# The compressed branch's steps one take earlier in a two-block fp32 layer kernel

## The chip, the cores and the metric

One NeuronCore of a Trainium2 chip runs the whole program. The metric is the device time of one execution in microseconds; for several executions the median is given.

## The reference

256 tokens of width 1024 pass a first block and then two layers of a second kind. All is float32.

```python
def first_block(x, ...):
    h = rms_norm(x, norm_mix_g)
    (f_q, f_k, f_v, f_f, n_q, k_c, v_c, k_s, v_s, k_w, v_w, n_g, g_a, g_b) = split_cols(h @ w_in)
    out_a = from_heads(fox_attention(qa, ka, va, log_f)) @ w_fox_up          # 8 heads, forget gates
    kc = rms_norm(compress_blocks(k_c, cmp_k_w1, cmp_k_w2, cmp_k_pos), nsa_k_g)
    vc = compress_blocks(v_c, cmp_v_w1, cmp_v_w2, cmp_v_pos)
    out_b = from_heads(nsa_attention(qb, kc, vc, ks_, vs_, kw_, vw_, gates)) @ w_nsa_up
    x = x + (sigmoid(g_a) * out_a + sigmoid(g_b) * out_b) @ w_out
    return x + hierarchical_moe(rms_norm(x, norm_ffn_g), ...)                # 16 experts, 2 of one group of 4

def compress_blocks(t, w1, w2, pos):      # t: (B,S,G,dh); 15 overlapping blocks of 32 tokens, stride 16
    blk = t[:, idx] + pos[None, None, :, None, :]
    return gelu(blk.reshape(B, G, n_cmp, 32 * dh) @ w1) @ w2
```

nsa_attention adds three branches with sigmoid gates: over the compressed keys, over selected blocks (at 256 tokens all blocks are selected), and over a window. The second block has two hybrid layers (a gated linear recurrence and a sliding-window attention).

## The kernel before, in words

**Takes and pieces.** The weights lie in HBM as half panels of 128x2048 (1 MB). SP loads them in a fixed order into a ring of four slots (`sp_program`, L532); load n waits until all that was read from load n - 4 is used. A half panel is cut into four pieces of 128x512. ScalarE makes each piece's high part (`copy` into `w_hi`, L1955) and VectorE its low part (`tt` into `w_lo`, L414), so that TensorE can multiply in three passes (`mm3`, L541 to L543). Two pieces are one take: take t uses pieces 2t and 2t + 1, and `feed(2 * t + AHEAD)` with AHEAD = 9 makes all pieces up to number 2t + 8 during take t. A `w_hi` buffer comes free through `taken`.

Takes 0 to 23 (T_Z) compute the columns of the first projection in six panels of four takes, with tokens on the partitions: tile 0 (tokens 0 to 127) in bank 0 and tile 1 in bank 1. In panel 0 TensorE runs the four takes for tile 0 first and then the four for tile 1. At the end of a panel ScalarE copies bank 0 to `zin` (`out_free[0]`, which TensorE waits for before the next panel) and VectorE bank 1. Takes 24 to 39 (T_GATE) are 24 matmuls each, 256 columns wide; takes 40 to 47 multiply with the two up matrices; takes 48 to 55 with w_out; then come the routing and the experts.

**What is done beside the takes.** `beside_block1` (L162) lists, for each take, the small steps that run on every engine in that take: attention blocks ("jobs") with scores, weigh, turn and values, and the steps 0 to 12 of the compressed branch. `ATT_1` gives each job's takes; job 6 has its scores in take 27, job 7 in 29, job 8 in 31, job 9 in 33, job 10 in 35, job 11 in 37, with weigh and turn two takes on and values two more. Per take, the engines run:

- TensorE: the take's matmuls, then the steps in the order of the list (`behind`, L1070);
- VectorE: first `log_in`, `weigh` and `scores_out` of this take, then the feed, then the rest (`behind`, L1840). `weigh_now` is the same function as `weigh` in this last part;
- ScalarE: the feed, `turn_out`, `scores_out` (the exponentials), the copy of a finished pair of gate rows, then the rest (`behind`, L2228). Each engine works strictly through its list and stands at every wait;
- GpSimd: small roots (`rstd_pow`, L426).

Two raw halves of each of the compressed branch's two first matrices come through the ring too, as loads 18, 19, 21 and 22. Loads 22 and 23 wait for `cmp_mm` 3, loads 25 and 26 for `cmp_mm` 4; load 21 waits for the four pieces of load 17 (68 to 71).

**The compressed branch.** TensorE's `compress` (L737), VectorE's (L1407), ScalarE's (L2056) and GpSimd's (L2384) share the step numbers; all of TensorE's use bank 7. TensorE raises `cmp_mm` after every step but 2.

- 0 and 1: TensorE transposes the raw keys (0) and values (1) into bank 7; VectorE copies them in four pieces to `kv2` (L1412) and raises `cmp_v`. TensorE's step 1 waits for `cmp_v` 1. Step 0 waits for `side` 9, set by `nsa_side` 3 of take 26.
- 2: VectorE adds the positions in eight instructions into `blk` (in `buf_d`), which GpSimd has zeroed (`cmp_z`).
- 3 and 4: TensorE multiplies the blocks with the first and second half of w1, 32 matmuls each (L757).
- 4 on ScalarE: GELU of the sum. 5: transposes. 6: second matrices (L770), VectorE's norm with GpSimd's root. 7: the key side. 8: scores (L780), softmax on VectorE and ScalarE. 9, 10: transposes of the probabilities, waiting for `cmp_f` of `cmp_weigh`. 11, 12: the values (L795).

`fx` and `fsum` (forget gates by pair of heads, used in takes 12 to 20) lay in `buf_d`, so the zeroing had to wait for the last forget-attention block. `buf_b` is first written otherwise by `nsa_side` 0 in take 22.

Of the kernel before, what the change touches and what calls it, by code (L numbers as in the profile page):

```python
# [14 lines left out]
P = 128  # L15
S = 256
# [3 lines left out]
HD = 64  # L20
# [66 lines left out]
FOX_JOBS, L1_JOBS = 4, 12  # L87
# [74 lines left out]
def beside_block1():  # L162
    table = {3: [("lower", 0)], 5: [("fox_sums", 0)], 7: [("fox_norms", 0)], 9: [("fox_sums", 1), ("fox_q", 0)],
             11: [("forget", 0), ("fox_norms", 1)], 12: [("log_in", 0), ("nsa_gates", 0)], 13: [("fox_k", 0)],
             20: [("win_sums", 0)], 21: [("win_norms", 0)], 22: [("nsa_side", 0), ("nsa_side", 1)],
             23: [("nsa_side", 2)], 24: [("slc_sums", 0)], 25: [("slc_norms", 0)], 26: [("nsa_side", 3)]}
    at_takes(table, list(enumerate(ATT_1)))
    for take, step in ((28, 0), (29, 1), (30, 2), (31, 3), (34, 4), (35, 5), (36, 6), (37, 7), (38, 8), (39, 9),
                       (40, 10), (41, 11), (42, 12)):
        table.setdefault(take, []).append(("compress", step))  # L170

    for take, job in ((31, 7), (39, 11)):
        table[take].remove(("weigh", job))
    table[30].insert(table[30].index(("compress", 2)), ("weigh_now", 7))
    table[38] += [("weigh_now", 11), ("cmp_weigh", 0)]
    for take, name, arg in ((39, "gate_on", 0), (41, "gate_on", 1), (43, "up_split", 0)):
        table.setdefault(take, []).append((name, arg))
    return table
# [55 lines left out]
def build(nc, panels, x_in, prm_in, lay_in, pre_in, post_in, c0_in, c1_in, c2_in, out):  # L234
    ctx = ExitStack()
    with ctx:
        V, A, T, G = nc.vector, nc.scalar, nc.tensor, nc.gpsimd
        pe, dve, act, pool, sp = Queue(T), Queue(V), Queue(A), Queue(G), Queue(nc.sync)
# [32 lines left out]
        buf_b = sb("buf_b", 1024)  # L271
        at_k = col()
        keys = sb("keys", 2560)
        buf_c = sb("buf_c", 2048)
        buf_d = sb("buf_d", 2048)
# [18 lines left out]
        ps = ctx.enter_context(nc.psum_tensor("ps", [P, 8, 512], F32))  # L294
# [22 lines left out]
        g_row = buf_a[:, :]  # L317
        slc_k = zin[:, TT * ZA:TT * ZA + S]
        ntri = c1("ntri")
        fx, fsum = buf_d[:, 0:2 * P], buf_d[:, 2 * P:2 * P + S]  # L320
        cq = stat[:, 112:128].rearrange("p (a h) -> p a h", a=TT)
        ng = stat[:, 128:176].rearrange("p (a c h) -> p a c h", a=TT, c=3)
        kv2 = buf_c[:, 0:1024].rearrange("p (c g t) -> p c g t", c=2, g=2)
# [12 lines left out]
        def sem(name):  # L336
# [26 lines left out]
        value_mm, value_out, value_hi = sem("value_mm"), sem("value_out"), sem("value_hi")  # L363
        cmp_mm, cmp_v, cmp_a, cmp_z, cmp_blk, cmp_ms, cmp_rs, cmp_n, cmp_s, cmp_f = (
            sem("cmp_" + n) for n in ("mm", "v", "a", "z", "blk", "ms", "rs", "n", "s", "f"))
# [777 lines left out]
        def dve_program():  # L1143
# [247 lines left out]
            def cmp_weigh(_):  # L1391
# [12 lines left out]
                settle()  # L1404
                tt(sc3, sc3, bc(fc, CMP_PAD), ALU.mult).then_inc(cmp_f, 1)

            def compress(step):  # L1407
                if step in (0, 1):
                    dve.wait_ge(cmp_mm, step + 1)
                    for g in range(2):  # L1410
                        for jp in range(2):
                            i = V.tensor_copy(kv2[jp * HD:(jp + 1) * HD, step, g, 0:S - jp], ps[g * HD:(g + 1) * HD, 7, jp:S])  # L1412
                    i.then_inc(cmp_v, 1)
                elif step == 2:
                    dve.wait_ge(cmp_v, 2)
                    dve.wait_ge(cmp_z, 2)
                    for c in range(2):
                        pos = prmc(("pos_k", "pos_v")[c])
                        for g in range(2):
                            even = kv2[:, c, g, :].rearrange("p (n m j) -> p m n j", n=16, j=2)[:, :, :, 0]  # L1420
                            tt(blk[c][:, 0:8, g, 0:N_CMP], even[:, :, 0:N_CMP], bc(pos[:, 0:8], N_CMP),
                               ALU.add).then_inc(cmp_blk, 1)
                            tt(blk[c][:, 8:16, g, 0:N_CMP], even[:, :, 1:N_CMP + 1], bc(pos[:, 8:16], N_CMP),
                               ALU.add).then_inc(cmp_blk, 1)
                elif step == 5:
                    dve.wait_ge(cmp_mm, 5)
                    V.tensor_copy(scr[:, 512:768], ps[:, 7, 0:256]).then_inc(cmp_v, 1)
                elif step == 6:
                    kcn, sq, ss = scr[0:64, 768:832], scr[0:64, 832:896], stat[0:64, 288:289]
                    dve.wait_ge(cmp_mm, 6)  # L1430
                    for g in range(2):
                        V.tensor_copy(vc_bd[g * 32:(g + 1) * 32, g * HD:(g + 1) * HD], ps[g * 32:(g + 1) * 32, 7, 64:128])
                    V.tensor_copy(kcn, ps[0:64, 7, 0:64]).then_inc(cmp_v, 1)
                    dve.wait_ge(cmp_v, 4)
                    dv(tt(sq, kcn, kcn, ALU.mult))
                    settle()
                    dv(V.tensor_reduce(ss, sq, AX, ALU.add))
                    settle()
                    rstd_in(ss, ss, HD).then_inc(cmp_ms, 1)
                    dve.wait_ge(cmp_rs, 1)  # L1440
                    ts(kcn, kcn, ss, None, ALU.mult).then_inc(cmp_n, 1)
                elif step == 7:
                    dve.wait_ge(cmp_mm, 7)
                    for g in range(2):
                        i = ts(kc_bd[g * HD:(g + 1) * HD, g * 32:(g + 1) * 32], ps[0:64, 7, g * 32:(g + 1) * 32],
                               prmc("nk_g")[0:64, :], None, ALU.mult)
                    i.then_inc(cmp_v, 1)
                elif step == 8:
                    sc = scr[:, 1024:1536]
                    sc3 = sc.rearrange("p (h n) -> p h n", n=CMP_PAD)  # L1450
                    mx = stat[:, 320:336]
                    dve.wait_ge(cmp_mm, 8)
                    tt(sc, ps[:, 7, :], c1("cmp"), ALU.add).then_inc(cmp_v, 1)
                    dve.wait_ge(cmp_v, 6)
                    dv(V.tensor_reduce(mx, sc3, AX, ALU.max))
                    settle()
                    tt(sc3, sc3, bc(mx, CMP_PAD), ALU.subtract).then_inc(cmp_s, 1)
                elif step >= 11:
                    a = step - 11
                    dst = z3[:, a, ZNQ:ZNQ + 512]  # L1460
                    dve.wait_ge(cmp_mm, step)
                    dve.wait_ge(value_out, value_sums[a])
                    tt(dst, dst, ps[:, 7, :], ALU.add).then_inc(cmp_v, 1)
                    cmp_sums[0] += 1
# [352 lines left out]
            def pre_los(l, a, c):  # L1817
# [7 lines left out]
                     "slc_norms": lambda _: head_norms(HEADS_SLC, 4), "nsa_side": nsa_side, "qf_bound": qf_bound,  # L1825
                     "log_in": log_in, "scores_out": scores_out, "weigh": weigh, "weigh_now": weigh, "cmp_weigh": cmp_weigh, "values_out": values_out,
                     "up_split": up_split, "att_split": att_split, "hg_turn": hg_turn,
                     "compress": compress, "rope": rope, "swa_sides": swa_sides, "level": level, "head_norm": head_norm,
                     "head_scale": head_scale}

            def steps(t):
# [25 lines left out]
            for t in range(T_Z, T_GATE):  # L1857
                steps(t)
                i, step = divmod(t, 4)
# [15 lines left out]
            for t in range(T_UP, T_OUT):  # L1875
                which, i = divmod(t - T_UP, 4)
# [5 lines left out]
                g = [gates[:, (8 * n + 2 * i) * S:(8 * n + 2 * i + 2) * S] for n in range(2)]  # L1882
# [68 lines left out]
        def act_program():  # L1951
# [300 lines left out]
            for t in range(T_Z, T_GATE):  # L2252
                feed(2 * t + AHEAD)
                steps(t, "turn_out")
                i, step = divmod(t, 4)
                if step == 3:
                    n = Z_ORDER[i]
                    cols = PIECE if n < 5 else Z5
                    act.wait_ge(tok_mm, i + 1)
                    copy(z3[:, 0, n * 512:n * 512 + cols], ps[:, 0, 0:cols]).then_inc(out_free[0], 1)  # L2260
                steps(t, "scores_out")
                behind(t)
            for t in range(T_GATE, T_UP):
# [3 lines left out]
                if f:  # L2267
                    c = (4 * n + 2 * b) * S
# [3 lines left out]
            for t in range(T_UP, T_OUT):  # L2272
                which, i = divmod(t - T_UP, 4)
# [26 lines left out]
            for l in range(LAYERS):  # L2300
# [10 lines left out]
                for t in range(t0, t0 + L2_TAKES - 3):  # L2311
# [14 lines left out]
                    elif L_QF <= r < L_IH and (r - L_QF) % 2:  # L2326
                        j, n = divmod(r - L_QF, 8)
                        b = n // 2 % 2
                        c = (4 * j + 2 * b) * S
# [26 lines left out]
        def pool_program():  # L2356
# [10 lines left out]
            def norm_root(a):  # L2367
                pool.wait_ge(norm_ms, a + 1)
                rstd_pow(stat[:, 2 + a:3 + a]).then_inc(norm_rs, 1)
# [12 lines left out]
                    rstd_pow(stat[:, s0:s0 + TT * n]).then_inc(head_rs, 1)  # L2382

            def compress(step):  # L2384
                if step == 0:
                    pool.wait_ge(value_out, FOX_JOBS)
                    G.memset(buf_d[:, :], 0.0).then_inc(cmp_z, 1)
                    G.memset(buf_c[:, 1024:1216], 0.0).then_inc(cmp_z, 1)
                elif step == 6:
                    pool.wait_ge(cmp_ms, 1)  # L2390
                    rstd_pow(stat[0:64, 288:289]).then_inc(cmp_rs, 1)

# [20 lines left out]
            po(G.memset(minus_half[:, :], -0.5))  # L2413
            pool.wait_ge(po.sem, po.n)
            po(G.memset(fx, 0.0))
            norm_root(0)
            norm_root(1)
            feed(5)
# [204 lines left out]
```

## Time and profile before

| | us |
|---|---|
| median of 3 runs | 1034.82 |
| lowest, highest | 1032.77, 1040.07 |
| profiled execution, its time | 1036.86 |
| profiled execution, its span | 1035.1 |

The span runs from the first to the last instruction; the time is taken around it. In rows of a timeline, the columns are start and busy time in us, engine, line, operation, destination<-source and shape, count, and in brackets how long the engine had been idle and what ended that. Matmuls overlap, so the distance of two starts is what one costs, not its busy time. On VectorE and ScalarE successive starts overlap by about 0.1 us as well.

### The profile page before, as it was taken

What the parts mean: (1) busy time and instruction counts of PE and PEld (TensorE: products, weight loads), DVE (VectorE), ACT (ScalarE), POOL (GpSimd) and SP (SyncE); (2) the same over time, 40 slices, a digit from 0 to 9 for tenths busy, and PEclk for the clock granted to TensorE, in tenths of its full rate; (3) what the DMA queues carried; (4) which work ended last, traced back from release to release, by engine and by line L of the source; (5) the groups of instructions that cost most, each with busy time, mean ns of one, the idle gap of its engine ahead of it and who ended that gap; (6) DMA issues with size and microseconds to landing.
All of it is one profiled execution on the core that took longest, in us unless ns stands there. A gap on an engine that the chain in (4) does not pass through costs nothing.

```text
span 1035.1 us, 16491 instructions
## 1 busy us (share of the span) xinstructions
PE 1006.2 (97%) x6087; PEld 863.6 (83%) x6087; DVE 838.2 (81%) x1653; ACT 666.5 (64%) x1351; POOL 54.7 (5%) x48
## 2 busy tenths in 40 slices
PE   5999999999999999999999999999999999999997
PEld 4888878887887888877879999888887999988886
DVE  5889867867999999999979777796668887598584
ACT  5476555547889888897855676735456477753552
POOL 0202000002004020010000000000100000000010
PEclk9999999999999999999999999999999999999999
DMA  8543253333999999999964443333354434234321
GB/s 346 192 175 123 86 233 130 141 145 112 391 365 374 392 350 381 366 339 366 384 241 164 163 148 139 101 140 127 112 194 177 170 122 160 90 129 150 117 91 41
DMA packets 30178, 211.31 MB, mean 204 GB/s; under 512 B 3728, under 2 KB 3856, under 8 KB 5136
## 3 DMA queue, kind: packets, MB, share of 16 engines
q1 hardware_dynamic: 28368, 205.01, 53.2%
q10 hardware_dynamic: 1728, 5.21, 1.3%
q8 instruction: 51, 0.84, 0.3%
q14 instruction: 31, 0.25, 0.1%
HBM read 209.16 MB, written 1.05 MB: 203 GB/s over the span
## 4 chain that ended last, share of the span: by engine, by line
PE 72%; DVE 15%; DMA 6%; ACT 4%; issue 2%; POOL 0%; ACTq 0%; DVEq 0%; POOLq 0%; SPq 0%
PE ps L541 19%; PE ps L543 18%; PE ps L542 18%; DVE w_lo L414 10%; DMA ring<-in_panels 5%; PE ps L1023 4%; PE ps L546 4%; PE ps L703 2%; PE ps L733 2%; ACT w_hi L1955 1%; DMA g_in<-in_prm 1%; PE ps L1011 1%; PE ps L757 1%; DVE op_rows L414 1%; DVE buf_d L1605 1%
## 5 line engine op out<-in xcount | busy, mean ns | idle before, releaser
L414 DVE TENSOR_TENSOR w_lo<-ring,w_hi 128x512 fp32r<-128x512 f32 x760 | 481.1, 689 | 84.8 <-ACT w_hi L1955 83.3
L1955 ACT ACTIVATE w_hi<-ring 128x512 fp32r<-128x512 f32 x760 | 427.4, 621 | 139.7 <-PE ps L543 106.9
L541 PE MATMUL ps<-w_hi,op_rows 128*128 128x512 f32 (+2 forms) x800 | 316.1, 395 | 7.2 <-DVE op_rows L414 3.6
L543 PE MATMUL ps<-w_hi,op_rows 128*128 128x512 f32 (+2 forms) x800 | 309.0, 386 | 0.0
L542 PE MATMUL ps<-w_lo,op_rows 128*128 128x512 f32 (+2 forms) x800 | 308.2, 385 | 0.0
L541 PEld LDWEIGHTS ps<-w_hi,op_rows 128*128 128x128 f32 x800 | 151.3, 189 | 41.0 <-DVE w_lo L414 5.9
L543 PEld LDWEIGHTS ps<-w_hi,op_rows 128*128 128x128 f32 x800 | 151.2, 189 | 30.9
L542 PEld LDWEIGHTS ps<-w_lo,op_rows 128*128 128x128 f32 x800 | 151.6, 190 | 27.5
L541 PE MATMUL ps<-op_rows,w_hi 128*128 128x256 f32 x544 | 158.5, 291 | 0.0
L542 PE MATMUL ps<-op_rows,w_hi 128*128 128x256 f32 x544 | 153.8, 283 | 0.0
L543 PE MATMUL ps<-op_rows,w_lo 128*128 128x256 f32 x544 | 153.7, 283 | 0.0
L541 PEld LDWEIGHTS ps<-op_rows,w_hi 128*128 128x128 f32 x544 | 104.0, 191 | 3.7 <-issue 1.1
L542 PEld LDWEIGHTS ps<-op_rows,w_hi 128*128 128x128 f32 x544 | 104.1, 191 | 0.0
L543 PEld LDWEIGHTS ps<-op_rows,w_lo 128*128 128x128 f32 x544 | 104.0, 191 | 0.0
L2001 ACT ACTIVATE s_buf<-s_buf,stat 128x256 f32<-128x256 f32 (+1 forms) x112 | 49.6, 444 | 61.7 <-DVE stat L417 61.7
L426 POOL TENSOR_TENSOR stat<-stat,minus_half 128x1 f32<-128x1 f32 (+4 forms) x22 | 26.1, 1188 | 771.8 <-DVE stat L420 615.5
L1023 PEld LDWEIGHTS ps<-gates 128*128 128x128 f32 (+2 forms) x448 | 48.8, 180 | 2.8 <-issue 0.7
L1023 PE MATMUL ps<-gates 128*128 128x64 f32 (+2 forms) x448 | 48.0, 261 | 0.0
L1955 ACT ACTIVATE zin<-ps 128x512 f32<-128x512 f32 (+2 forms) x32 | 17.6, 564 | 34.7 <-PE ps L543 20.3
L2397 POOL TENSOR_TENSOR op_rows<-gates,op_rows 128x256 fp32r<-128x256 f32 x16 | 23.3, 1464 | 192.6 <-ACT op_rows L1955 192.6
L414 DVE TENSOR_TENSOR gates<-gates,buf_d 128x512 f32<-128x512 f32 (+1 forms) x36 | 25.3, 743 | 7.8 <-PE ps L1023 7.8
L417 DVE TENSOR_SCALAR s_buf<-s_buf,stat 128x128 f32<-128x128 f32 x112 | 29.5, 340 | 1.0
(250 smaller groups left out, 1054.8 us busy)
## 6 DMA issues: line engine op xcount, KB each, us to landing
ring<-in_panels SPq DMA_DIRECT2D x194, 1024.0 KB, 5.9
cst<-in_c ACTq DMA_DIRECT2D x1, 1229.0 KB, 6.7
buf_a<-in_pre ACTq DMA_DIRECT2D x2, 512.0 KB, 6.1
keys<-in_post ACTq DMA_DIRECT2D x2, 512.0 KB, 5.1
out<-x_tok SPq DMA_DIRECT2D x2, 512.0 KB, 2.6
cst<-in_c ACTq DMA_DIRECT2D x1, 960.0 KB, 6.4
x_tok<-in_x SPq DMA_DIRECT2D x1, 512.0 KB, 4.8
x_tok<-in_x ACTq DMA_DIRECT2D x1, 512.0 KB, 5.0
```

Source lines behind the costliest of these rows:

```text
L414: return V.tensor_tensor(o, a, b, op)
L417: return V.tensor_scalar(o, a, s1, s2, op0, op1) if op1 is not None else V.tensor_scalar(o, a, s1, None, op0)
L426: return G.tensor_tensor(o, o, e.to_broadcast(list(o.shape)), ALU.pow)
L541: T.matmul(o, l[0], r[0], start=start, stop=False)
L542: T.matmul(o, l[0], r[1], start=False, stop=False)
L543: return T.matmul(o, l[1], r[0], start=False, stop=stop)
L546: return T.transpose(o, a, ident[0:n, 0:n])
L703: m = T.matmul(ps[:, 2 + e, lo:lo + n], q(a)[half, :], k[half, 0:n], start=True, stop=plain)
L1023: m = T.matmul(ps[0:rows, 2 + 2 * j + lv % 2, n * HD:(n + 1) * HD], k_of(j)[:, n * P:n * P + rows], late[:, n * per:(n + 1) * per, :], sta ...
L1955: return A.activation(o, a, ACT.Copy, scale=scale)
L2001: i = A.activation(sc[:, lo:lo + n], sc[:, lo:lo + n], ACT.Exp, bias=ng_[:, c:c + 1], accum_out=sm[:, c:c + 1])
L2397: G.tensor_tensor(o[1], rows_in[:, c:c + 256], o[0].bitcast(F32), ALU.subtract).then_inc(xg_lo, 1)
```

## The change

Steps 0 to 8 of the compressed branch stand one take earlier. VectorE's copies of steps 0 and 1 become steps of their own (`compress_in`) which stay in takes 28 and 29, first in what VectorE does behind the feed. Job 7's weigh is back in its own take 31. The zeroing is done at the program's start on GpSimd, for which `fx` and `fsum` move to `buf_b`. ScalarE copies panel 0's tile 0 in take 0, not in take 3.

```diff
-    for take, step in ((28, 0), (29, 1), (30, 2), (31, 3), (34, 4), (35, 5), (36, 6), (37, 7), (38, 8), (39, 9),
+    for take, step in ((27, 0), (28, 1), (29, 2), (30, 3), (33, 4), (34, 5), (35, 6), (36, 7), (37, 8), (39, 9),
                        (40, 10), (41, 11), (42, 12)):
         table.setdefault(take, []).append(("compress", step))
-
-    for take, job in ((31, 7), (39, 11)):
-        table[take].remove(("weigh", job))
-    table[30].insert(table[30].index(("compress", 2)), ("weigh_now", 7))
+    for take, step in ((28, 0), (29, 1)):
+        table[take].insert(0, ("compress_in", step))
+
+    table[39].remove(("weigh", 11))
     table[38] += [("weigh_now", 11), ("cmp_weigh", 0)]
...
-        fx, fsum = buf_d[:, 0:2 * P], buf_d[:, 2 * P:2 * P + S]
+        fx, fsum = buf_b[:, 0:2 * P], buf_b[:, 2 * P:2 * P + S]
...
+            def compress_in(c):
+                dve.wait_ge(cmp_mm, c + 1)
+                for g in range(2):
+                    for jp in range(2):
+                        i = V.tensor_copy(kv2[jp * HD:(jp + 1) * HD, c, g, 0:S - jp], ps[g * HD:(g + 1) * HD, 7, jp:S])
+                i.then_inc(cmp_v, 1)
+
             def compress(step):
-                if step in (0, 1):
-                    dve.wait_ge(cmp_mm, step + 1)
-                    for g in range(2):
-                        for jp in range(2):
-                            i = V.tensor_copy(kv2[jp * HD:(jp + 1) * HD, step, g, 0:S - jp], ps[g * HD:(g + 1) * HD, 7, jp:S])
-                    i.then_inc(cmp_v, 1)
-                elif step == 2:
+                if step == 2:
...
                 i, step = divmod(t, 4)
-                if step == 3:
+                if step == (3 if i else 0):
                     n = Z_ORDER[i]
                     cols = PIECE if n < 5 else Z5
                     act.wait_ge(tok_mm, i + 1)
...
             def compress(step):
-                if step == 0:
-                    pool.wait_ge(value_out, FOX_JOBS)
-                    G.memset(buf_d[:, :], 0.0).then_inc(cmp_z, 1)
-                    G.memset(buf_c[:, 1024:1216], 0.0).then_inc(cmp_z, 1)
-                elif step == 6:
+                if step == 6:
...
             po(G.memset(fx, 0.0))
+            G.memset(buf_d[:, :], 0.0).then_inc(cmp_z, 1)
+            G.memset(buf_c[:, 1024:1216], 0.0).then_inc(cmp_z, 1)
             norm_root(0)
```

## Rows read from the trace of the kernel before

**Rows 1.** The page's busy times: engine, us (share of the span), instructions
```profile
PE 1006.2 (97%) x6087; PEld 863.6 (83%) x6087; DVE 838.2 (81%) x1653; ACT 666.5 (64%) x1351; POOL 54.7 (5%) x48
```

**Rows 2.** TensorE's waits up to 260 us: who for whom, us, times, longest
```profile
PE ps L546 <- DVE s_buf L417: 1.9, 3, 0.9
PE ps L546 <- issue: 1.1, 1, 1.1
PE ps L541 <- ACT zin L1955: 0.5, 1, 0.5
```

**Rows 3.** TensorE's timeline, takes 27 to 38
```profile
112.40 0.87 PE L546 MATMUL ps<-ident,s_buf 128*128 128x128 f32 x6 [0.64 <-DVE s_buf L417]
...
114.05 0.38 PE L541 MATMUL ps<-op_rows,w_hi 128*128 128x256 f32 x1
...
117.03 0.38 PE L546 MATMUL ps<-ident,zin 128*128 128x128 f32 x2
...
132.81 3.67 PE L757 MATMUL ps<-ring,buf_d 128*64 128x256 f32 x32 [0.40 <-DVE buf_d L414]
...
144.82 0.39 PE L541 MATMUL ps<-op_rows,w_hi 128*128 128x256 f32 x1
...
169.86 1.89 PE L780 MATMUL ps<-buf_c,buf_b 128*128 128x64 f32 x16
```

**Rows 4.** VectorE's timeline, takes 27 to 38
```profile
110.13 2.21 DVE L417 TENSOR_SCALAR s_buf<-s_buf,stat 128x128 f32<-128x128 f32 x4
...
114.17 1.02 DVE L1308 SCALAR_TENSOR_TENSOR s_buf<-cst,ps 128x384 f32<-128x384 f32 x2 [0.63 <-PE ps L703]
...
116.35 1.29 DVE L414 TENSOR_TENSOR w_lo<-ring,w_hi 128x512 fp32r<-128x512 f32 x2
...
117.89 1.72 DVE L1412 COPY buf_c<-ps 64x256 f32<-64x256 f32 x4
...
130.55 2.21 DVE L414 TENSOR_TENSOR buf_d<-buf_c,prm 128x120 f32<-128x120 f32 x8
...
136.05 1.29 DVE L414 TENSOR_TENSOR w_lo<-ring,w_hi 128x512 fp32r<-128x512 f32 x2
...
161.54 0.43 DVE L1432 COPY buf_c<-ps 32x64 f32<-32x64 f32 x2
...
163.72 0.17 DVE L1334 RECIPROCAL stat<-stat 128x4 f32<-128x4 f32 x1
...
165.04 1.29 DVE L414 TENSOR_TENSOR w_lo<-ring,w_hi 128x512 fp32r<-128x512 f32 x2
...
171.79 0.69 DVE L414 TENSOR_TENSOR scr<-ps,cst 128x512 f32<-128x512 f32 x1 [0.47 <-PE ps L780]
...
173.85 0.17 DVE L1334 RECIPROCAL stat<-stat 128x4 f32<-128x4 f32 x1
```

**Rows 5.** GpSimd's timeline, the zeroing
```profile
109.87 1.81 POOL L2387 MEMSET buf_d<- 128x2048 f32 x1 [7.81 <-DVE fox_lo L414]
```

**Rows 6.** ScalarE's timeline, GELU; then the chain's line of one block's exponentials
```profile
151.66 1.28 ACT L2060 ACT_TABLE_LOAD   x1 [0.67 <-PE ps L757]
...
153.23 1.14 ACT L1955 ACTIVATE w_hi<-ring 128x512 fp32r<-128x512 f32 x2
...
127.31 1.88 ACT s_buf L2001 x8
```

**Rows 7.** SP's issues of three ring loads; the later two (issue, then us to landing)
```profile
136.82 1.28 SPq L532 DMA_DIRECT2D ring<-in_panels  x3
...
L532 SPq DMA_DIRECT2D ring<-in_panels x2: 432/432/433, 137.2 to 137.7; - x2
...
DMA to landing us min/median/max: 6.9/8.5/10.2
```

**Rows 8.** TensorE's timeline at 782.68; windows 782 to 786 (last columns PEclk, DMA, GB/s)
```profile
782.68 0.76 PE L541 MATMUL ps<-w_hi,op_rows 128*128 128x512 f32 x1 [1.84 <-DVE op_rows L414]
...
782.00:786.00 4.00, 3.32 (x8) 2.67 (x9) 3.96 (x8) 1.84 (x6) 0.55 (x1) 0.57 0.55 229
```

More of the change, by code:

```diff
@@ L1827, in dve_program @@
                      "up_split": up_split, "att_split": att_split, "hg_turn": hg_turn,
-                     "compress": compress, "rope": rope, "swa_sides": swa_sides, "level": level, "head_norm": head_norm,
+                     "compress_in": compress_in, "compress": compress, "rope": rope, "swa_sides": swa_sides, "level": level, "head_norm": head_norm,
                      "head_scale": head_scale}
```

## The prediction

> **What bounds the kernel now.** I read the busy shares first, then what TensorE waited for, then the timelines of the four engines between 95 and 195 us, where the moved steps run, and last the transfers into the weight ring. TensorE (PE) is busy 97% of the span [rows 1]: a change here can only win idle gaps of PE or add new ones. PE's work is not altered, only its order. The waits name the gaps within reach [rows 2]: the turns of attention blocks on VectorE's weighing (1.9 us in three places: the longest, 0.9, is turn 7, turn 5 is 0.64 in [rows 3], and 0.37 is left for turn 10), the first tile of panel 1 on ScalarE's copy (0.46), compress 3 on the blocks (0.40, in [rows 3]) and 1.1 before compress 9 (shown as issue; VectorE's cmp_weigh ends there). That is 3.9 us in all, 0.4% of the time; with the 0.1 or so that each restart costs, some 4.6. A measurement of this kernel can tell about 1% from no change, so the gain cannot be large whatever the change does; the question is what the new order makes PE wait for.
>
> I name two instants. X is where PE is through with scores 6, behind take 27 (114.05 in the trace); W is the start of take 32 (132.81 + 3.60 = 136.4, as compress 3 ends there). PE needs 2.98 for the 24 matmuls of a take (114.05 to 117.03), 1.65 for turn and scores together (112.40 to 114.05), so about 0.8 each and for values too, 0.15 (estimate) for compress 0 or 1, and 3.6 for compress 3 or 4 [rows 3].
>
> **Panel 0's copy at take 0.** ScalarE copied bank 0 behind the pieces of take 3, and PE stood 0.46 for it [rows 2]. Bank 0 is complete before the first half of tile 1, and ScalarE then waits for PE to release a piece buffer, so the copy lies in an idle gap. Gain 0.46 (between 0, if a VectorE wait replaces it, and 0.6 with the restart). I take -0.45.
>
> **Zeros at the start.** The 128x2048 memset ran on GpSimd from 109.87 to 111.68 [rows 5], and weigh 5's four multiplications, issued at 110.13, took 2.21 [rows 4]; in weigh 10 the whole step from 163.72 to 165.04, reciprocal included, takes 1.32. So 1.2 us of VectorE go, and with them the 0.64 for which PE waited at turn 5 [rows 3]. At the start nothing runs on VectorE before the first norm, so the memset costs nothing there. fx and fsum move to buf_b at no cost. -0.65 (between -0.8 and 0).
>
> **Compress 0 to 3.** VectorE's order at take 28 is scores_out 6, the feed, then compress_in 0. scores_out starts at X + 0.12 and holds VectorE 2.18 (114.17 to 116.35), the feed 1.21 (1.29 less the overlap of starts), the four copies 1.72 [rows 4]: cmp_v rises at X + 5.2. But PE, which ran compress 0 at X, is through take 28 at X + 3.1 and wants compress 1, which waits for that same cmp_v, since both use bank 7. It stands 2.15 us, and take 29 with everything behind it waits with it. Before, a whole take lay between. In return VectorE builds the blocks (2.14) by X + 12.0, before PE is at compress 3 (X + 13.8), and weigh 7, now in take 31, is done at X + 17.6 against X + 21.3 for turn 7. So the 0.87 at turn 7 and the 0.40 at compress 3 go, with 0.3 of restarts. Take 32 starts at X + 22.9 instead of X + 22.36: **+0.55**. (Bounds: 0 if VectorE comes to the copy a microsecond sooner, +1.3 if the removed waits come back elsewhere.)
>
> **Compress 4 and the ring.** SP issues loads in order. Load 22, which compress 4 reads, stands behind load 21, and that behind piece 71 of load 17, which VectorE makes first thing in feed(32). In the trace feed(32) starts at 136.05 [rows 4] and the three loads go out from 136.82 on [rows 7], load 21 by piece 71 (0.77 behind the start of the feed), 22 and 23 by compress 3. Load 22 (137.2) landed 6.9 later at 144.1, load 23 (137.7) 10.2 later at 147.9 [rows 7]; PE came to compress 4 only behind take 34, at 144.82 + 3.0 = 147.8 [rows 3]. In the new order scores 8 ends right at W, since compress 3 went ahead of take 31: scores_out 8 then runs W + 0.1 to 2.3, the feed's first piece releases load 21 at W + 3.05, and load 22 lands 7.3 behind that, at W + 10.35. PE is at compress 4 behind take 33, at W + 8.45 (144.82 less 136.4). It stands **1.9 us**. The least is 0, if load 22 lands as fast as a load alone; the most 3.
>
> **What ScalarE's order adds.** Compress 4 now stands in take 33, so ScalarE takes the GELU ahead of feed(34), turn_out 8 and the exponentials of block 9; before, it did these while PE was still in take 34 and compress 4. Let E be the end of compress 4. GELU with its table load is over at E + 1.73 (151.66 to 153.23 [rows 6]), two pieces 1.05, turn_out's 768 columns 0.7 (estimate from the 0.52 of a 512-column piece), exponential's table 1.28, exponentials 1.88 [rows 6]: E + 6.65; weigh 9 takes 1.32: E + 8.05. PE, with take 34, compress 5, take 35 and values 8, is at turn 9 at E + 7.0. **+1.1**. Next, compress 6 holds VectorE 2.18 (161.54 to 163.72 [rows 4], the wait for GpSimd's root within) and can't start before PE's part is through at E + 10.5 (turn 9 from E + 8.1, scores 10, and 0.65, an estimate, for the small matmuls). It now stands ahead of scores_out 10 and no longer behind it: scores_out 10 ends at E + 14.85, exponentials at E + 16.85, weigh 10 at E + 18.2, where PE is at turn 10 at E + 17.3. 0.95, where there was 0.37 [rows 2]: **+0.55**. Then compress 8 (1.73 on PE, then 2.06 on VectorE, 171.79 to 173.85 [rows 3, 4]) stands ahead of scores_out 11: from the end of scores 11 it is 1.75 + 2.06 + 2.18 + 0.15 + 1.88 + 1.35 = 9.4 to the end of weigh 11, and PE needs 1.73 + 2 x 3.0 + 0.8 = 8.5 to turn 11: **+0.95**. cmp_weigh comes behind it as before, so the 1.1 before compress 9 stays. These three are bounded below by 0 and above by about double. Takes 40 on keep their order.
>
> By the Trainium skill's page "ScalarE: Activation LUTs", section "What ACT_TABLE_LOAD costs", each switch of tables also drains for about 1.4 us; turn 9 would then come 2.8 us later still. The trace has 1.28 for the load and the activation right behind it, so no drain is in the sum.
>
> **Sum.** -0.45 - 0.65 + 0.55 + 1.9 + 1.1 + 0.55 + 0.95 = +3.95, say **+4.0 us**. The profiled execution took 1036.86 (span 1035.1 and 1.8 around it), 2.0 above the median of the three runs; the sum is a difference, so I add it to the median: 1034.8 + 4.0 = **1038.8 us**.
>
> **Rivals.**
> *The gains come and the new waits do not* (12%). The copies and the load are in time: then all of 0.45, 0.65, 1.6 (turn 7, compress 3), 0.4 (turn 10) and 1.2 (compress 9) are won, 4.3 us: 1030.5, faster than before. For it speaks that pieces are made four takes ahead, so that no short delay on VectorE or ScalarE starves PE of weights. It decides at compress 1: cmp_v would have to stand by X + 3.1, and I see no way past scores_out 6 and the feed.
> *The two early waits are real, the later ones are covered* (20%). ScalarE and VectorE may catch up in takes 34 to 39, or load 22 land sooner: -0.45 - 0.65 + 0.55 + between 0 and 1.9, thus 1034.3 to 1036.2. For it: each late step is under 1.2 us, and a shift of some tenths in one queue moves it. Against: each delay makes the following one.
> *The clock falls* (10%). At 782.68 PE had stood 1.84 us after a thin stretch of transposes, and for the following 4 us the granted clock was 0.57 [rows 8], so about half the work of that stretch was lost, 1.7 us. It is the lower level, 1.2 GHz, for most of it. My waits of 2.15 and 1.9 are of this length, but dense matmuls stand on both sides, so I hold it less likely. Both falling: 1038.8 + 3.4 = 1042.2. The Trainium skill's page "TensorE: Matmul & The Clock Gate", section "What's actually happening", has the clock follow how busy the array has just been; by that rule such a wait is a risk, and this row agrees.
> *The forecast itself* has 58%; its own range is 1036 to 1041.5.
>
> **How the numbers follow.** The three runs before spread from 1032.8 to 1040.1, so a median of the new kernel can lie some 2 us off either way. The range takes in the second rival and most of the third, and leaves the gains-only case outside: 1033.0 to 1043.0. Faster by over 1% would be below 1024.5, beyond every gap there is to win: 0.02. Slower by over 1%, above 1045.2, needs both clock drops and a high draw: 0.05. Within 1%: 0.93.
>
> **What would show it.** Right: weigh 5 near 1.3 us and no wait at turn 5; no ScalarE wait of PE at 27; a PE wait of some 2 us on VectorE's buf_c copies (about 116 to 119); one of some 2 us before the second group of 32 compress matmuls, released by a ring load or shown as issue; waits of about 1 us at turns 9, 10 and 11. Wrong: PE passes compress 1 or compress 4 without a wait; load 22 goes out before piece 71; or the span falls below that of before.

## The result, and the profile after

| | before | after |
|---|---|---|
| median of the runs, us | 1036.62 (9 runs, 1032.77 to 1040.07) | 1044.96 (9 runs, 1042.09 to 1045.98) |
| profiled execution, us | 1036.86 | 1043.80 |
| its span, us | 1035.1 | 1042.0 |
| mean granted clock over the timed executions | 0.9974 (52 other runs, those beside the experiments on two chips; none is on record for the nine) | 0.9933 (9 runs) |

The new kernel takes 1.0084 times as long, [1.0070, 1.0098]: 8 us by the medians, where 4.0 were forecast, and 2 us beyond the upper end of the range. The busy times of PE are those of [rows 1]. VectorE is busy 2.0 us less, of which 1.2 are the multiplications that the memset had slowed:

```profile
PE 1006.4 (97%) x6087; PEld 863.1 (83%) x6087; DVE 836.2 (80%) x1653; ACT 661.8 (64%) x1351; POOL 44.8 (4%) x48
```

GpSimd's 9.9 us less are not the memset's, which takes 1.81 in both: its sixteen multiplications into op_rows, in a part that the change doesn't touch, took 23.3 us before and 13.7 after, and over the ten profiles of this document GpSimd is busy between 44.8 and 57.9, ScalarE between 661.8 and 668.9.

PE does the same work, so the time is in its gaps. Its waits between 100 and 200 us (who for whom, us in all, times, longest), against [rows 2]:

```profile
PE ps L757 <- DMA ring<-in_panels: 3.4, 1, 3.4
PE ps L546 <- DVE s_buf L417: 3.0, 3, 1.2
PE ps L546 <- DVE buf_c L1411: 2.0, 1, 2.0
PE ps L546 <- issue: 1.2, 1, 1.2
PE ps L733 <- DVE zin L414: 0.2, 1, 0.2
```

Two new ones: the copies of compress_in (2.0) and a ring load before compress 4 (3.4). The turns of attention blocks rose from 1.9 to 3.0. PE's timeline has each in its place, against [rows 3]:

```profile
112.46 0.44 PE L546 MATMUL ps<-ident,zin 128*128 128x128 f32 x2
...
117.73 0.44 PE L546 MATMUL ps<-ident,zin 128*128 128x128 f32 x2 [1.97 <-DVE buf_c L1411]
...
126.50 3.67 PE L757 MATMUL ps<-ring,buf_d 128*64 128x256 f32 x32
...
147.52 4.99 PE L757 MATMUL ps<-ring,buf_d 128*64 128x256 f32 x32 [3.41 <-DMA ring<-in_panels]
...
160.69 0.88 PE L546 MATMUL ps<-ident,s_buf 128*128 128x128 f32 x6 [1.23 <-DVE s_buf L417]
...
170.95 0.87 PE L546 MATMUL ps<-ident,s_buf 128*128 128x128 f32 x6 [0.82 <-DVE s_buf L417]
...
182.45 0.87 PE L546 MATMUL ps<-ident,s_buf 128*128 128x128 f32 x6 [0.94 <-DVE s_buf L417]
...
184.52 1.03 PE L546 MATMUL ps<-ident,scr 128*64 128x128 f32 x4 [1.20 <-issue]
```

X is now 112.46 (compress 0 follows take 27 at once), 1.6 us sooner than before; compress 3 at 126.50 waits for nothing. Read the two groups of 32 matmuls side by side: the same work takes 3.67 at 126.50 and 4.99 at 147.52. The windows say why (us, then busy time of PE, PEld, DVE, ACT, POOL with instructions, PEclk, DMA share, GB/s):

```profile
118.00:122.00 4.00, 4.00 (x36) 3.55 (x35) 3.89 (x13) 0.92 (x2) 0.00 (x0) 1.00 0.36 147
146.00:150.00 4.00, 2.48 (x12) 1.64 (x14) 0.39 (x2) 0.00 (x0) 0.00 (x0) 0.60 0.48 201
184.00:188.00 4.00, 3.48 (x18) 3.40 (x19) 1.62 (x3) 2.32 (x3) 0.00 (x0) 0.57 0.00 0
```

Behind the 3.41 wait the clock granted over 146 to 150 is 0.60, for most of it the lower of its two levels, 1.2 GHz. It is 0.57 again over 184 to 188, where PE stood 0.94 and 1.20 close together. Behind the 1.97 wait, at 118 to 122, it stays full here.

VectorE's timeline around the first wait, and at the start of take 32, against [rows 4]:

```profile
109.24 1.01 DVE L417 TENSOR_SCALAR s_buf<-s_buf,stat 128x128 f32<-128x128 f32 x4
...
114.76 1.29 DVE L414 TENSOR_TENSOR w_lo<-ring,w_hi 128x512 fp32r<-128x512 f32 x2
115.96 1.72 DVE L1411 COPY buf_c<-ps 64x256 f32<-64x256 f32 x4
...
137.93 1.29 DVE L414 TENSOR_TENSOR w_lo<-ring,w_hi 128x512 fp32r<-128x512 f32 x2
```

Weigh 5's multiplications take 1.01 instead of 2.21, and turn 5 no longer waits. The copies end at 117.68, X + 5.2, as worked out. The feed at 137.93 is feed(32); its first piece releases SP's three loads. SP's issues, all three and then the last two (issue, then us to landing), against [rows 7]:

```profile
138.70 1.28 SPq L532 DMA_DIRECT2D ring<-in_panels  x3
...
DMA to landing us min/median/max: 4.8/8.3/10.3
...
L532 SPq DMA_DIRECT2D ring<-in_panels x2: 432/432/432, 139.1 to 139.5; - x2
...
DMA to landing us min/median/max: 8.3/9.3/10.3
```

Scores 8 ended at 135.63 (W), so load 21 went out at W + 3.07; W + 3.05 was worked out. Load 22 (139.1) landed 8.3 later, where it had taken 6.9 before.

Where the 6.9 us of the span are, by three instants of PE's timelines:

| us | before | after | difference |
|---|---|---|---|
| start to X | 114.05 | 112.46 | -1.59 |
| X to the start of take 40 | 63.69 | 72.75 | +9.06 |
| take 40 to the end | 857.4 | 856.8 | -0.6 |

The last line can't be read as an effect of the change. Takes 40 on are ordered alike in all ten kernels of this document and took 854.2 to 859.0 us in their profiles. The profile before had the clock at 0.57 over 236 to 240 and 782 to 786, that of after at full there, but it holds most of the fall that began at 184: take 40 takes 4.08 us (185.21 to 189.29) and not 2.92 (177.74 to 180.66). In the medians such luck is averaged out; they differ by 8.3 us and not by 6.9.

### The profile page after: what moved, and what is told of

It reads as the page before. It is cut to its first block, busy times and chain, and to the rows that moved or that the text cites. A ratio compares the mean times of both kernels' runs of the same rounds, so it can differ in the third digit from the quotient of the medians.

```text
span 1042.0 us, 16491 instructions
## 1 busy us (share of the span) xinstructions
PE 1006.4 (97%) x6087; PEld 863.1 (83%) x6087; DVE 836.2 (80%) x1653; ACT 661.8 (64%) x1351; POOL 44.8 (4%) x48
## 4 chain that ended last, share of the span: by engine, by line
PE 64%; DVE 18%; DMA 10%; ACT 5%; issue 2%; POOL 1%; ACTq 0%; DVEq 0%; SPq 0%; POOLq 0%
PE ps L541 16%; PE ps L543 16%; PE ps L542 16%; DVE w_lo L414 11%; DMA ring<-in_panels 9%; PE ps L1023 4%; PE ps L546 3%; PE ps L703 2%; ACT w_hi L1956 2%; PE ps L733 2%; DVE op_rows L414 1%; DMA g_in<-in_prm 1%; PE ps L757 1%; DVE buf_d L1606 1%; PE ps L1011 1%
## 5 line engine op out<-in xcount | busy, mean ns | idle before, releaser
L546 PE MATMUL ps<-ident,scr 128*128 128x128 f32 (+2 forms) x107 | 16.7, 293 | 10.9 <-DMA ident<-in_ident 8.7
```

Source lines behind the costliest of these rows:

```text
L546: return T.transpose(o, a, ident[0:n, 0:n])
```

## The experiments

My theory after the result: the places are those forecast, the load wait is larger by its landing time, and the rest is clock lost behind the waits. The rivals: that the early steps (0 to 3), or the memset and the early copy, carry part of the loss; or that the load wait comes of the ring's order and goes with another. Each of the eight ran beside the kernel before on one chip, four on one and four on another.

| kernel | median, us | before there | ratio, 95% | mean clock | take 40 - X |
|---|---|---|---|---|---|
| steps all back (e1) | 1033.87 | 1034.46 | 0.9992 [0.9977, 1.0007] | 0.9976 | 63.67 |
| steps 4 to 8 back (e2) | 1035.60 | 1034.46 | 1.0009 [0.9993, 1.0025] | 0.9968 | 64.77 |
| ring order (e4) | 1048.66 | 1034.46 | 1.0126 [1.0103, 1.0149] | 0.9906 | 79.34 |
| products into the gap (e5) | 1041.81 | 1034.46 | 1.0065 [1.0042, 1.0088] | 0.9972 | 72.47 |
| copy in take 27 (e3) | 1041.67 | 1035.75 | 1.0054 [1.0036, 1.0071] | 0.9942 | 71.71 |
| piece 71 first (e6) | 1038.60 | 1035.75 | 1.0025 [1.0012, 1.0037] | 0.9963 | 69.12 |
| that, and GELU late (e7) | 1038.16 | 1035.75 | 1.0021 [1.0007, 1.0034] | 0.9955 | 68.27 |
| all three, 6 to 8 back (e9) | 1034.25 | 1035.75 | 0.9984 [0.9971, 0.9997] | 0.9969 | 63.33 |

**The zeros and the early copy alone (e1).**

```
-    for take, step in ((27, 0), (28, 1), (29, 2), (30, 3), (33, 4), ... (37, 8), (39, 9),
+    for take, step in ((28, 0), (29, 1), (30, 2), (31, 3), (34, 4), ... (38, 8), (39, 9),
...
+        if step < 2:
+            table[take].append(("compress_in", step))
...
+    table[30].insert(table[30].index(("compress", 2)), ("weigh_now", 7))
```

> Only the zeros at the start and panel 0's early copy; the compressed branch's steps and job 7's weigh stand where they stood before. My theory (all of the loss lies in the order of the steps): PE is about 1.5 us ahead of the kernel before by the end of scores 6, no new wait comes in, and the time is 1 to 2 us below the kernel before, ratio 0.998 to 0.999. Rival (moving buf_d's zeros or the early copy costs something of its own, later or at the start): the time is that of the kernel before or above it, ratio 1.000 to 1.003.

Measured: 0.6 us below before by the medians (ratio 0.9992, with 1 inside its interval). The waits at turn 5 and for ScalarE's copy are gone, and take 40 comes 63.67 behind X as before (63.69). The ratio lies between the two expected ranges. So these two parts cost at most 0.7 us, by the end of the interval, and whether they gain the 1.1 of the forecast the ratio cannot tell: it fits 1.1 and it fits 0. The loss is in the order of the steps.

**Steps 4 to 8 back, 0 to 3 early (e2).**

```
-    ... (30, 3), (33, 4), (34, 5), (35, 6), (36, 7), (37, 8), (39, 9),
+    ... (30, 3), (34, 4), (35, 5), (36, 6), (37, 7), (38, 8), (39, 9),
```

> The changed kernel with steps 4 to 8 back in takes 34 to 38; steps 0 to 3 stay one take early. My theory: the 2 us wait at compress 1 stays, the wait for the ring load before compress 4 is gone or below 0.5 us, so are those of about 1 us at turns 9 and 10, and TensorE's clock stays at its higher level from 140 to 190 us; the time is 0.5 to 1 us below the kernel before (-1.6 for zeros and copy, +0.8 for compress 1), ratio 0.9985 to 1.0005. Rival (the loss comes from the early steps 0 to 3, which shift scores 8 and so load 21): a wait of 2 us or more stays before compress 4 and the ratio is 1.003 or more.

Measured: 1.0009, just above the expected range of up to 1.0005, with an interval that reaches into it. Waits of PE from 100 to 200 us:

```profile
PE ps L546 <- DVE buf_c L1411: 2.0, 1, 2.0
PE ps L546 <- issue: 1.1, 1, 1.1
PE ps L733 <- DVE zin L414: 0.7, 1, 0.7
PE ps L546 <- DVE s_buf L417: 0.4, 1, 0.4
PE ps L757 <- DMA ring<-in_panels: 0.2, 1, 0.2
```

The wait at compress 1 is there in full, and the kernel costs only about 1 us against before, not clear of noise, since turn 7 and compress 3 no longer wait. Against e1, which has the zeros and the early copy but not the early steps, take 40 comes 1.1 us later behind X (64.77 against 63.67), and the medians differ by 1.7: that is the price of steps 0 to 3. Load 22 landed 8.2 after its issue here too, and PE, a take later, waited 0.2 for it: it was the take in between that had hidden the load. The difference to after, 1.0084 less 1.0009, or 7.8 us, belongs to steps 4 to 8. The rival that the early steps carry most of the loss falls.

**Another order of the ring (e4).** The halves that compress 4 reads are loaded right behind those of compress 3, so that load 22 stands earlier in SP's order.

```
-                out += [(2 * PN_CMP + i, 0, None) for i in (0, 2)]
-            if n == 9 and h == 0:
-                out += [(2 * PN_CMP + i, 0, None) for i in (1, 3)]
+                out += [(2 * PN_CMP + i, 0, None) for i in (0, 2, 1, 3)]
```

> The changed kernel with the two raw second halves (for compress 4) ordered in the ring right behind the first ones, ahead of the half panel of takes 36 and 37, so that compress 4 waits for the load released by piece 71 alone, issued 3.05 us behind the start of take 32 and landing 4.8 later, with TensorE there at 8.4. My theory: no load wait before compress 4, compress 4 takes 3.6 us and not 5.0, and what is left is the waits of about 1 us at compress 1 (2.0) and turns 9, 10, 11; 4.8 us below the changed kernel, 3 to 4 above the kernel before, ratio 1.003 to 1.004. Rival (ScalarE's order is the bound, and the load wait only hides it): less than 2 us below the changed kernel, ratio 1.006 or more.

Measured: 1.0126, worse than the change. The expectation missed a user of the ring. The half panel whose pieces ScalarE begins in feed(32) moved back behind those for compress 4, into the late group of three loads. ScalarE's only wait between 135 and 150 us:

```profile
ACT w_hi L1954 <- DMA ring<-in_panels: 11.6, 1, 11.6
```

then PE's longest wait from 100 to 200, and the window around it:

```profile
PE ps L731 <- DVE zin L1359: 6.2, 1, 6.2
```

```profile
144.00:156.00 12.00, 6.07 (x30) 4.08 (x32) 4.89 (x13) 4.59 (x13) 0.00 (x0) 0.57 0.40 166
```

The values of block 7 waited for VectorE's copy, VectorE stood behind the pieces, and ScalarE behind the load. The wait for a late load moved from PE to ScalarE and from there back to PE, at a higher price: another order of the same three loads makes another user late.

**Products into the gap (e5).** Fourteen products of 512 columns into a free bank before compress 4 keep PE busy while load 22 lands; everything else is as in after.

```
                     pe.wait_ge(cmp_blk, 8)
+                    if h:
+                        pe.wait_ge(out_free[1], 8)
+                        idle_products(14, 1)
```

> The changed kernel with 14 dummy products of 512 columns (about 3.2 us) on a free bank ahead of compress 4, where TensorE waits for the load anyway. My theory (the clock falls because TensorE stood 3.4 us, and that costs about 1.4 us): the start of compress 4 is unchanged at some 12 us behind the start of take 32, but the granted clock stays at 1.0 and its 32 matmuls take 3.6 us instead of 5.0; 1.4 us below the changed kernel, ratio to the kernel before 1.006 to 1.0075. Rival (the clock fell by chance or its cost is hidden behind ScalarE's GELU chain): the same as the changed kernel, ratio 1.008 to 1.009.

Measured: 1.0065 against 1.0084, as expected, though the two intervals overlap and six runs don't part them; the mean clock is 0.9972 against 0.9933. The trace is what tells. PE's timeline and windows:

```profile
148.79 3.67 PE L760 MATMUL ps<-ring,buf_d 128*64 128x256 f32 x32
```

```profile
118.00:122.00 4.00, 4.00 (x25) 4.00 (x23) 3.89 (x13) 0.00 (x0) 0.00 (x0) 0.63 0.39 164
146.00:150.00 4.00, 4.00 (x25) 2.88 (x25) 1.71 (x5) 0.00 (x0) 0.00 (x0) 1.00 0.81 336
```

Compress 4's matmuls take 3.67 and not 4.99, with no gap ahead and the clock at full: the 1.3 us are the clock's, and the gap is what costs them. The other profiles agree: in e3, where PE waits 3.21 before compress 4, its 32 matmuls take 5.23, and in the six profiles without a gap above 0.3 there (before, e1, e2, e6, e7, e9) they take 3.67. The load wait itself is still paid, in products. In this profile the clock fell at 118 to 122, behind the wait at compress 1. From X to the end of scores 7 it is 12.43 here, and 10.97 in after, with the same wait of 1.97 in both; the difference, 1.5 us, is the price of one fall, near the 1.7 read from [rows 8].

**Piece 71 ahead of everything in take 32 (e6).** VectorE makes the pieces that release load 21 before scores_out 8 instead of behind it.

```
             for t in range(T_GATE, T_UP):
+                if t == 32:
+                    feed(72)
                 ahead(t)
```

> The changed kernel with one piece fed sooner: VectorE makes the low part of piece 71 at the head of take 32, ahead of scores_out 8, in time in which it stood idle for 4.3 us. Load 21 goes out some 3.5 us sooner and loads 22 and 23 with it; ScalarE's order is as it was. My theory (the load behind piece 71 is the cause of the 3.4 us wait, and that wait of the fallen clock): the wait before compress 4 is below 0.5 us, its 32 matmuls take 3.6 us, the waits of about 1.2, 0.8 and 0.9 us at turns 9, 10 and 11 stay; 4 to 5 us below the changed kernel, ratio to the kernel before 1.003 to 1.0045. Rival (ScalarE, standing in its GELU step, is the bound and the wait of PE only moves to the turns): turn 9 waits 3 us or more and the ratio stays at 1.006 or more.

Measured: 1.0025, 1.0084 less 0.0059, or 6.1 us won back, the largest single share and more than the 4 to 5 expected. The three loads go out from 136.18 on, 0.42 ahead of W (136.60 here) and no longer 3.07 behind it, and the wait before compress 4 is gone:

```profile
PE ps L546 <- DVE s_buf L417: 3.0, 3, 1.2
PE ps L546 <- DVE buf_c L1411: 2.0, 1, 2.0
PE ps L546 <- issue: 1.2, 1, 1.2
PE ps L733 <- DVE zin L414: 1.0, 2, 0.7
```

The wait of 3.4 and the 1.3 of slow matmuls make 4.7; the rest is within the intervals of the two ratios. The three turns keep their 3.0, so they don't come from the load wait.

**That, and the GELU behind the exponentials (e7).** On top of the last edit ScalarE takes compress 4's GELU one take later, behind the exponentials of block 9.

```
+    table[34].append(("gelu", 0))
...
-                if step == 4:
-                    act.wait_ge(side, 9)
...
+            def gelu(_):
+                act.wait_ge(side, 9)
```

> The previous kernel (piece 71 sooner), and ScalarE's GELU of step 4 in take 34, behind feed, turn_out 8 and the exponentials of block 9, where it stood before the change; TensorE's compress 4 stays in take 33. My theory (the wait at turn 9 is ScalarE standing in its list at compress 4): the wait at turn 9, 1.2 us, goes, compress 5 waits below 0.5 us for GELU; those at turns 10 and 11 stay, since they come from VectorE's steps 6 and 8 ahead of scores_out; 1 us below the previous kernel, ratio to the kernel before 1.002 to 1.0035. Rival (the wait at turn 9 is an echo of the load, or VectorE's): no gain over the previous kernel.

Measured: 1.0021 against 1.0025; the intervals don't part them. The trace does: turn 9 no longer waits, the other two do, and compress 5 waits 0.2 for the GELU.

```profile
PE ps L548 <- DVE s_buf L419: 1.8, 2, 0.9
PE ps L548 <- ACT scr L2074: 0.2, 1, 0.2
```

Take 40 - X is 0.85 shorter (68.27 against 69.12). The cause of turn 9's wait is so shown, its size in the medians is not.

**compress_in 0 at the end of take 27 (e3).** The change as it is, with VectorE's first copies ahead of scores_out 6.

```
-    for take, step in ((28, 0), (29, 1)):
-        table[take].insert(0, ("compress_in", step))
+    table[27].append(("compress_in", 0))
+    table[29].insert(0, ("compress_in", 1))
```

> The changed kernel with VectorE's copy of step 0 in take 27, ahead of scores_out 6, and nothing else. My theory (PE's 2.0 us before compress 1 is scores_out 6 and a feed standing ahead of the copy): that wait is gone; scores_out 6 runs 2 us later, so turn 6 waits about 0.5 us and compress 3 about 0.4; 1.0 to 1.3 us below the changed kernel with all later waits as they are, ratio to the kernel before 1.006 to 1.008. Rival (the later waits stretch by what is won here, since load 21 hangs on VectorE): the ratio stays at 1.0075 to 1.009 and the wait before compress 4 grows to 4 us or more.

Measured: 1.0054, better than expected. PE's waits from 100 to 200 us:

```profile
PE ps L546 <- DVE s_buf L417: 3.7, 4, 1.2
PE ps L757 <- DMA ring<-in_panels: 3.2, 1, 3.2
PE ps L546 <- issue: 1.2, 1, 1.2
PE ps L757 <- DVE buf_d L414: 0.3, 1, 0.3
```

The wait at compress 1 is gone, and about half comes back: 0.71 at turn 6 (the three turns are now four) and 0.34 at compress 3. Take 40 comes 1.04 sooner behind X; the ratio gained 0.0030, or 3.1 us, more than the trace has. A fall of the clock that needs no longer follow the 1.97 wait would fill some of that, and the mean clock rose from 0.9933 to 0.9942; with six runs I leave it open.

**The version that takes all three (e9).** The copies in take 27, piece 71 first and the late GELU, with steps 6 to 8 back in takes 36 to 38, so that 0 to 5 alone stand early.

```
-    ... (33, 4), (34, 5), (35, 6), (36, 7), (37, 8), (39, 9),
+    ... (33, 4), (34, 5), (36, 6), (37, 7), (38, 8), (39, 9),
```

> All three mends together (copy 0 in take 27, piece 71 sooner, GELU behind the exponentials), and steps 6 to 8 back in takes 36 to 38. My theory: no wait above 0.6 us at compress 1, compress 4, turns 6 to 9; turn 10 (0.4) and compress 9 (1.1) wait as in the kernel before; the higher clock throughout; 1.5 to 2.5 us below the kernel before, ratio 0.9975 to 0.9988, better than both kernels. Rival (each step taken early shifts its wait to another place, so that nothing can be won): ratio 0.9995 to 1.002.

Measured: 1034.25, ratio 0.9984 [0.9971, 0.9997], 1.5 us below before. Its waits of PE:

```profile
PE ps L548 <- issue: 1.1, 1, 1.1
PE ps L735 <- DVE zin L416: 0.7, 1, 0.7
PE ps L548 <- DVE s_buf L419: 0.7, 1, 0.7
PE ps L759 <- DVE buf_d L416: 0.3, 1, 0.3
PE ps L548 <- ACT scr L2074: 0.2, 1, 0.2
```

Turns 10 and 11 wait no more once compress 6 and 8 stand behind scores_out 10 and 11 again. Two waits differ from the expectation: the 0.7 is turn 6, above the 0.6 allowed, and the 0.37 of turn 10 in the kernel before is gone too, which I can't explain. The ratio is the lowest of all and the only one whose interval lies below 1. But the intervals of e1 and, barely, e2 overlap it: e1 leaves all steps where they stood and has 1033.87 for its 1034.46, and behind X the two differ by 0.34 us in the traces (63.33 against 63.67). So e9 is faster than the kernel before; that the early order adds anything to the zeros and the early copy isn't shown. 3.0 us of waits are left in this stretch. A version with a bank of its own for compress 1, which would take the first wait away without moving the copies, wasn't tried.

## Why the prediction was half right

**The early gains** (-0.45, -0.65). The waits went as forecast: turn 5's 0.64 with the shorter multiplications, ScalarE's 0.46, of which 0.2 came back as a wait for VectorE's zin copy (0.2, in PE's waits up to 100 us). X came 1.6 us sooner, which holds also the 0.15 of compress 0 that now runs behind it; about 0.5 of the 1.6, restarts included, I can't place. In time, e1 neither confirms nor denies them.

**Compress 0 to 3** (+0.55). Confirmed in place, and in size within its bounds. The wait was 1.97 for 2.15; turn 7 and compress 3 no longer waited; from X to W it is 23.17 against 22.37 before, +0.80. The run with steps 4 to 8 back, set against e1, prices the early steps at 1.1 us by the traces.

**Compress 4 and the ring** (+1.9). This is the step that failed first. All its stations were right: load 21 at W + 3.07, PE at compress 4 at W + 8.48 (147.52 less 3.41, less 135.63), 3.05 and 8.45 forecast. The landing was not. I took 6.9 from a single row [rows 7] and used it as if exact. The second of these three loads landed 6.8 to 7.0 behind its issue in before, e1, e6, e7 and e9, where the group goes out within 0.5 of W, and 8.1 to 8.3 in after, e2, e3 and e5, where it goes out some 3 behind W; the first (4.7 to 4.9) and the third (10.1 to 10.3) hardly moved. So the wait was 3.41, +1.5. The bound of 3, too, had been set too low; reading it from the landing of the third load would have covered this.

**Turns 9, 10 and 11** (+1.1, +0.55, +0.95). 1.23, 0.82 where 0.37 had been (+0.45), and 0.94: +2.62 for 2.60. The late GELU took away turn 9's wait alone, which shows that mechanism. The other two went in e9, which puts steps 6 to 8 back; it also moves the first copy, but e3, with that copy moved alone, keeps them (0.81 and 0.94), so they come of steps 6 to 8. Which of the three steps makes which wait was worked out and not taken apart. ScalarE's timeline has the step that starts the first; there is again no gap behind the table load:

```profile
152.58 1.28 ACT L2061 ACT_TABLE_LOAD   x1 [10.30 <-PE ps L757]
153.88 0.38 ACT L2061 ACTIVATE scr<-ps 128x256 f32<-128x256 f32 x1
154.16 1.15 ACT L1956 ACTIVATE w_hi<-ring 128x512 fp32r<-128x512 f32 x2
```

**The sum.** The waits alone give +4.0 + 1.5 = 5.5. Of the 8.3 in the medians 2.8 are left, and I put them down to the clock. The mean clock fell by 0.0041, which over 1040 us is 4.3 us of full clock: about an upper bound, since PE stood during part of it, and a rough one, since the clock of before is that of other executions. In the profile the segments say much the same: of the +9.06 from X to take 40, 0.80 + 3.41 + 1.23 + 0.45 + 0.94 + 0.1 (compress 9) + 0.23 (the values at 180.63) are waits and early steps, 1.3 are compress 4's slow matmuls, 0.3 the start of the second fall (184.52 to 185.21, against 177.38 to 177.74 before), and 0.3 are left for restarts. With the 1.2 that the second fall costs in take 40, the two falls cost 2.8 in this profile.

The forecast of 1038.8 is 6.2 us below the median of 1044.96: 4.3 are the sum, 1.8 the base, since 1034.8 was the median of three runs and that of nine is 1036.6. On that base the range would have ended at 1044.8.

**The rivals.** Gains-only (12%) and late steps covered (20%) fall: no new wait was covered. The clock's fall (10%) came true, though in the profile behind compress 4 and compress 9 and not behind compress 1, and leaving it out of the sum was the step that failed second. I had its price about right, 1.7 for 1.5, and its probability wrong, because I read [rows 8] as the fruit of thin work around the wait. Dense matmuls on both sides did not protect: the wait of 1.97 at compress 1 has them, and a fall followed it in four of six profiles. Above all I made it an alternative to the forecast, when it belonged into the sum: two waits of 2 us at even odds and 1.6 us each are +1.6 in the mean. That, and a load wait reaching up to the third load's landing (10.2 for 6.9, 3.3 more), would have put the forecast at up to 1043.7 and, with both falls whole at 1.7 each, at 1045.5. The even odds are hindsight: the rows of before had one such wait.

**The chances.** Within 1% held 93%, and the ratio is within it. Slower by over 1% had 5%; that it was so near is again the clock.

## What to carry to other kernels

When a step is moved a slot forward, follow every in-order queue behind it, and ask of each thing that it reads when that was issued, not only whether it was there before: here one slot of slack had hidden the landing of a 1 MB load and ScalarE's stand before the GELU, and one line that put the releasing piece first won back 6 of 8 us. Where the forecast has PE standing 2 us or more, put a fall of the clock into the sum with its odds, and when a group of loads goes out at another moment than in the trace, give the landing of each a range that reaches to the next one's. Only with its prerequisites moved along, and with steps 6 to 8 left late, did the early order come out ahead of the kernel before, by 0.16%, and not by more than the zeros and the early copy alone may give.

## What the runs showed of the hardware that I had not expected

- The clock's answer to a gap isn't settled by the gap. The same wait of 1.97 us at compress 1, with the same matmuls on both sides, was followed by a fall in e4, e5, e6 and e7 and by none in after and e2. Likewise the waits of 0.94 and 1.20 at turn 11 and compress 9 were followed by one in after and e3 and by none in e4, e5, e6 and e7. The window of e6 (the columns as above), to be held against the first one of after:

```profile
118.00:122.00 4.00, 4.00 (x24) 3.84 (x23) 3.92 (x11) 0.00 (x0) 0.00 (x0) 0.57 0.27 113
```

  In the same 4 us 24 matmuls ran here and 36 in after. The Trainium skill's page "TensorE: Matmul & The Clock Gate", section "What's actually happening", says that the moment at which the clock rises at a kernel's start varies from run to run of the same kernel. It says so of the rise; these traces show such a spread for the fall, behind gaps of 2 us.
- Of three loads issued 0.4 us apart, the second lands at one of two times, 6.8 to 7.0 or 8.1 to 8.3 us behind its issue, and the first hardly varies. In before, 138 to 146, and in after, 142 to 146, the three keep the DMA engines busy for over 0.8 of the time at 348 to 434 GB/s, so they share one rate, and the third lands 10.2 or 10.3 behind its issue in both; how much of the second goes before the third is what differs. The late landing came in each of the four profiles that keep the ring's order and issue the group 3 us behind W, so it is hardly chance. The moment alone doesn't decide it: e4, whose group of another order also goes out some 3 us behind W (139.6, W at 136.55), has 4.7, 6.9 and 8.9. What does, no run shows.
- A memset on GpSimd doubled the time of VectorE's multiplications beside it: 2.21 with it [rows 4], 1.01 without. The first of the four took the loss: in before it began at 110.13, took 1.63 us and ended at 111.76, just behind the memset's end at 111.68. At the start the memset takes the same 1.81 us and is over long before VectorE's first work at 6.93 and GpSimd's next at 7.17:

```profile
1.14 1.81 POOL L2413 MEMSET buf_d<- 128x2048 f32 x1
...
7.17 0.55 POOL L426 TENSOR_TENSOR stat<-stat,minus_half 128x1 f32<-128x1 f32 x1 [4.02 <-DVE stat L420]
```

  The Trainium skill's page "SBUF — State Buffer", section "SBUF: two separate sides", has GpSimd and VectorE, when VectorE runs an operation in a mode that uses two ports, take turns on one pair of ports for a whole instruction. The first multiplication's end right behind the memset's agrees with it, but no run here parts the port from another cause.
